# Small experts in 32-row slots, their outputs summed in PSUM expert by expert, with eleven weight slots instead of nine

## The chip, the cores and the metric

The kernel runs on one core of a Trainium2 chip. The metric is the device time of one execution in microseconds (us); lower is better. The engines are PE (TensorE), DVE (VectorE), ACT (ScalarE), POOL (GpSimd) and SP (SyncE, which here only starts the weight loads).

## The reference, cut to what matters

The model has two layers, 256 tokens of width 1024, all in fp32. Each layer has a first block (a token mixer and a mixture of 32 small experts) and a second block. The change touches the mixture of the 32 small experts. In outline:

```python
# x: [256, 1024]; E = 32 experts, hidden width F = 256, two experts per token
top2, p = route(x)                      # two expert numbers and two weights a token
y = 0
for e in range(32):
    h = silu(x @ w_gate[e]) * (x @ w_up[e])        # 1024 -> 256
    y += weight_of(token, e) * (h @ w_down[e])     # 256 -> 1024, 0 for tokens that e isn't chosen for
x = layer_norm(x * alpha + y)
```

So 512 pairs of token and expert are computed, on average 16 rows an expert. With the reference's inputs no expert gets more than 26 rows in either layer (counted from the reference's routing).

## The kernel before

All weights are streamed from HBM once. `load_weights` (L3546) issues the loads in program order on SP's queue, into `weight_ring`, RING = 9 slots of 1 MiB; a load waits until PE has used the tile that stood in its slot before. A second buffer, `weights_high` (HIGHS = 3 slots), holds the rounded high parts of those weights that are multiplied as a sum of two rounded parts, such as the projection `w_o` ahead of the experts.

Each small expert has three tiles, `moe_w_gate`, `moe_w_up` and `moe_w_down`. They are loaded in the order gate(0), up(0), then gate(x+1), up(x+1), down(x) for each x, so that the last three of the 96 are up(31) (with gate(31)), down(30) and down(31).

`sparse_experts` (L2488 on) does one mixture. The 512 pairs are ordered by expert into 512 slots. DVE makes a 0/1 matrix `G` (tokens x slots). PE transposes it to `spread` (8 products, L2590), ACT and DVE copy that out of PSUM (L2655, L2669), PE gathers the tokens' columns into the slots (`e_xg`, 32 products at L2600, of which the last 20 wait for those copies). Idle products at L130 (`idle_products`) fill PE's waits. Then `SmallExperts` (L1926) goes over the 32 experts with windows of W = 64 slots. Its PE program for step x is, in order: `first(x+1)` (half of gate and up, L1986), `turn(x)` (transposes of the hidden rows, L2007), `turn_out(x-1)` (transposes of the output rows, L2026), `second(x+1)` (the other half, L1986), `third(x)` (down, L2017). The weights are the moving operand; the x window of 64 slots is the stationary one, and two column tiles of 64 stand side by side (up and gate, or the halves of down's 1024 columns). ACT copies the hidden part (L2087), the next x window (L2094) and the output rows (L2101) and does silu (L2098, with L2096 before it, which takes a silu of one column ahead); DVE multiplies (L2134) and writes the turned output rows to `e_outT` (L2116). `by_width` reads the expert's count and branches to a wide program if the count is over W.

`sum_slots` (L2683, 32 products of one column) sums the router's weight for each slot on PE, behind the first expert's gate and up. After the last expert the engines join, and a mixing stage brings the slots back to the tokens: PE transposes `e_outT` (L2737), ACT and DVE scale each slot by its weight and split it in two rounded parts (L2762, L2769), and PE multiplies them by `spread` (L2746). DVE then adds the result to `x` (L2775, in the second layer L2777). In the second layer `meanwhile` puts a split of two tiles for the block that follows (ACT L112, DVE L116) between the join and that add.

The loops of SP, ACT and DVE over the experts are hardware loops of six experts a turn; PE's is written out.

Of the kernel before, what the change touches and what calls it, by code (L numbers as in the profile page):

```python
# [50 lines left out]
class WeightRing:  # L51
# [4 lines left out]
    def __init__(self, core):  # L56
        self.nc = core.nc
        self.buf, self.lows = core.sb_twice("weight_ring", [P, RING, SLOT])
        self.spare, self.highs = core.sb_twice("weights_high", [P, HIGHS, SLOT])
        self.full = [core.new_sem(f"weights_full_{i}") for i in range(RING)]  # L60
        self.used = core.new_sem("weights_used")
        self.high_ready, self.split_ready = core.new_sem("high_parts_ready"), core.new_sem("weights_split")
        self.loaded = [0] * RING
        self.tiles = 0
        self.split_tiles = []
        self.plan = []

    def view(self, n, kt, cols):
        return self.buf[:, n % RING, 0:kt * cols].rearrange("p (k n) -> p k n", k=kt)
# [9 lines left out]
    def next(self, src, split=False):  # L79
# [4 lines left out]
        self.tiles += 1  # L84
        self.loaded[n % RING] += 16
# [1635 lines left out]
def claim_stream(c, n, gate, up, down):  # L1721
# [6 lines left out]
    for x in range(p0, p0 + 3 * n):  # L1728
        ring.loaded[x % RING] += 16
# [198 lines left out]
class SmallExperts:  # L1928

    W = 64  # L1930

    def __init__(self, c, p0, n, unroll, xg, outT, tiles, landed, used, cnt, off):
        self.c, self.p0, self.n, self.unroll, self.xg, self.outT = c, p0, n, unroll, xg, outT
        self.gate_tile, self.down_tile = tiles
        self.landed, self.used, self.cnt, self.off = landed, used, cnt, off
        assert unroll % 2 == 0
        self.x = c.S[:, 0, :, :].rearrange("p k t -> p (k t)")[:, 0:2 * KD * self.W].rearrange("p (b k s) -> p b k s", b=2, k=KD)
        self.wide_x = c.S[:, 1, :, :]
        flat = c.xT[:, :, :].rearrange("p k t -> p (k t)")
        self.out_rows = flat[:, 0:512]  # L1940
        self.wide_hidden = flat[:, 1024:2048].rearrange("p (b m t) -> p b m t", b=2, m=2)
        spare = c.spare_x[:, :, :].rearrange("p k t -> p (k t)")
        self.hidden = spare[:, 0:2 * self.W].rearrange("p (m s) -> p m s", m=2)
        self.primed = spare[:, 640:642]
        self.squashed_rows, self.hidden_rows = spare[0:self.W, 1536:1792], spare[:, 1792:2048]
        self.wide_squashed = spare[:, 1024:1536].rearrange("p (m t) -> p m t", m=2)
        self.windowed, self.squash_done, self.rows_ready = c.sig("small_window"), c.sig("small_squashed"), c.sig("small_hidden_rows")
        self.turned, self.hidden_ready = c.sig("small_turned"), c.sig("small_hidden")
        self.rows_copied, self.out_turned, self.written = c.sig("small_rows_copied"), c.sig("small_out_turned"), c.sig("small_written")
        self.wide_act, self.wide_dve = c.sig("wide_slots_act"), c.sig("wide_slots_dve")  # L1950
        self.each = {self.windowed: 1, self.squash_done: 1, self.rows_ready: 1, self.turned: 1, self.hidden_ready: 1,
                     self.rows_copied: 1, self.out_turned: 1, self.written: 1, self.wide_act: 2, self.wide_dve: 2}
# [6 lines left out]
    def of(self, signal, x, i, part=None):  # L1959

        each = self.each[signal]
        return signal.sem, each * self.unroll * i + (self.base[signal] + each * x + (each if part is None else part))

    def load_count(self, eng, x, i):
        return eng.value_load(self.cnt[0:1, bass.ds(x + self.unroll * i, 1)], min_val=0, max_val=TOK)

    def by_width(self, eng, x, i, small, wide, count=None):

        if count is None:
            count = self.load_count(eng, x, i)  # L1970
# [5 lines left out]
    def offset(self, eng, x, i):  # L1976
        return eng.value_load(self.off[0:1, bass.ds(x + self.unroll * i, 1)], min_val=0, max_val=SLOTS)

    def gate_and_up(self, x, k0, k1):
# [10 lines left out]
    def first(self, pe, x):  # L1990
        pe.wait_ge(*self.of(self.windowed, x, 0))
        if x >= 2:
            pe.wait_ge(*self.of(self.rows_ready, x - 2, 0))
# [7 lines left out]
    def turn(self, pe, x):  # L2001
        pe.wait_ge(*self.of(self.rows_ready, x, 0))
        if x >= 2:
            pe.wait_ge(*self.of(self.hidden_ready, x - 2, 0))
        blocks = self.hidden_rows.rearrange("s (f m) -> s m f", m=2)
        for m in range(2):
            last = self.c.nc.tensor.transpose(self.c.psum[:, 2 + x % 2, m * P:(m + 1) * P], blocks[:, m, :], self.c.ident[:, :])  # L2007
        last.then_inc(self.turned.sem, 1)

    def third(self, pe, x):  # L2010
        nc, psum, W = self.c.nc, self.c.psum, self.W
        pe.wait_ge(*self.of(self.hidden_ready, x, 0))
# [8 lines left out]
    def turn_out(self, pe, x):  # L2021
        pe.wait_ge(*self.of(self.rows_copied, x, 0))
        if x >= 2:
            pe.wait_ge(*self.of(self.written, x - 2, 0))
        for j in range(4):
            last = self.c.nc.tensor.transpose(self.c.psum[:, 6 + x % 2, j * P:(j + 1) * P], self.out_rows[:, j * P:(j + 1) * P], self.c.ident[:, :])  # L2026
        last.then_inc(self.out_turned.sem, 1)

    def wide_first(self, pe, x):
        nc, psum = self.c.nc, self.c.psum  # L2030
        pe.wait_ge(*self.of(self.wide_act, x, 0, 1))
        pe.wait_ge(*self.of(self.wide_dve, x, 0, 1))
        for a, bank in ((0, 0), (1, 2)):
# [455 lines left out]

# [1274 lines left out]
```

## Time and profile before

| | |
|---|---|
| time, median of 3 runs | 2324.22 us (2323.08 to 2326.17) |
| profiled execution: own time | 2319.28 us |
| profiled execution: span | 2317.6 us |
| mean granted TensorE clock | 0.977 |
| busy: PE / DVE / ACT / POOL | 93% / 35% / 29% / 3% of the span |
| HBM read | 605.11 MB |
| chain that ended last | PE 72%, DVE 12%, DMA 8% |

The span is what the trace covers; the execution's own time is 1.7 us longer. The two mixtures of small experts lie at about 140 to 410 us and 600 to 868 us of the span. A granted clock of 1.00 is TensorE's 2.4 GHz level and 0.50 the 1.2 GHz one; a stretch between them had some of both.

### The profile page before, as it was taken

Reading aid. Unit: us, or ns where it says so; the run is one execution under the profiler, and the core shown is the slowest. Engines: PE = TensorE matmul, PEld = TensorE weight load, DVE = VectorE, ACT = ScalarE, POOL = GpSimd, SP = SyncE. Lnnn points to the kernel's source line nnn. Section 1 sums busy time; section 2 is a strip of 40 time slices with the busy share of each in tenths; the row PEclk is TensorE's granted clock in tenths of the full one; section 3 lists DMA queues with packets and bytes.
Section 4 is the critical chain, followed back from the end, with each engine's and each line's share of the span. In section 5 each row is a group of like instructions: output and inputs, shape, how many; then the busy total and the mean of one; then the engine's idle time right before and its main releaser. Section 6 shows DMA issues by size and latency. Waiting matters only on the chain.

```text
span 2317.6 us, 48110 instructions
## 1 busy us (share of the span) xinstructions
PE 2148.5 (93%) x19825; PEld 1636.9 (71%) x19825; DVE 811.6 (35%) x1483; ACT 668.6 (29%) x1151; POOL 70.3 (3%) x122
## 2 busy tenths in 40 slices
PE   7899888988998889898999998989999999999997
PEld 6775445977754559887999897876667676676775
DVE  5541112655411126974566688540000000000002
ACT  4422222453322234554333346420000000000002
POOL 0100000101000002000000200000000000000000
PEclk9999999999999999999999999999999999999999
DMA  7439999622399996333454642418999999999993
GB/s 240 143 107 419 418 419 371 185 92 76 149 418 419 419 346 175 115 128 127 146 182 147 189 164 92 146 38 326 392 371 395 379 375 400 369 377 402 364 388 123
DMA packets 196758, 610.06 MB, mean 263 GB/s; under 512 B 11472, under 2 KB 87072, under 8 KB 163728
## 3 DMA queue, kind: packets, MB, share of 16 engines
q1 hardware_dynamic: 190688, 590.84, 67.8%
q0 software_dynamic: 5248, 13.25, 2.5%
q8 instruction: 210, 3.44, 0.6%
q10 hardware_dynamic: 560, 2.10, 0.2%
q14 instruction: 52, 0.43, 0.1%
HBM read 605.11 MB, written 1.05 MB: 262 GB/s over the span
## 4 chain that ended last, share of the span: by engine, by line
PE 72%; DVE 12%; DMA 8%; ACT 3%; issue 3%; DVEq 1%; SPq 0%; ACTq 0%; POOLq 0%
PE psum L2245 18%; PE psum L2250 12%; DMA weight_ring<-in_moe_w_up_dram 8%; PE psum L1986 7%; PE psum L137 7%; PE psum L139 7%; PE psum L138 7%; PE psum L2017 2%; DVE weight_ring_rounded L116 2%; PE psum L936 1%; DVE h_cf L3165 1%; ACT scores L970 1%; PE psum L2746 1%; PE psum L2282 1%; PE psum L2026 1%
## 5 line engine op out<-in xcount | busy, mean ns | idle before, releaser
L2245 PE MATMUL psum<-weight_ring,weights_high 128*32 128x512 f32 (+2 forms) x4608 | 478.1, 470 | 0.0
L2250 PE MATMUL psum<-weight_ring,weights_high 128*32 128x256 f32 (+1 forms) x2304 | 445.5, 346 | 0.0
L1986 PE MATMUL psum<-weight_ring,scores 128*64 128x256 f32 x2048 | 259.4, 395 | 51.1 <-issue 27.4
L2250 PEld LDWEIGHTS psum<-weight_ring,weights_high 128*32 128x32 f32 x2304 | 242.7, 110 | 54.8 <-issue 1.0
L1986 PEld LDWEIGHTS psum<-weight_ring,scores 128*64 128x64 f32 x2048 | 150.6, 141 | 160.1 <-issue 111.1
L2245 PEld LDWEIGHTS psum<-weight_ring,weights_high 128*32 128x32 f32 x4608 | 184.1, 110 | 85.1 <-issue 41.1
L2250 PE MATMUL psum<-weight_ring,xT_high 128*32 128x256 f32 x1056 | 232.2, 379 | 0.0
L2245 PE MATMUL psum<-weight_ring,xT_high 128*32 128x256 f32 (+1 forms) x2112 | 231.5, 486 | 0.0
L137 PE MATMUL psum<-xT_high_rounded,weights_high_rounded 128*128 128x256 f32 x768 | 218.0, 284 | 2.2 <-DVE xT_rounded L369 1.4
L139 PE MATMUL psum<-xT_high_rounded,weight_ring_rounded 128*128 128x256 f32 x768 | 217.1, 283 | 0.0
L2354 DVE TENSOR_TENSOR xT<-xT,psum 128x768 f32<-128x768 f32 (+1 forms) x24 | 21.8, 910 | 512.4 <-PE psum L2250 374.1
L138 PE MATMUL psum<-xT_rounded,weights_high_rounded 128*128 128x256 f32 x672 | 189.1, 281 | 0.0
L116 DVE TENSOR_TENSOR weight_ring_rounded<-weight_ring,weights_high_rounded 128x2048 fp32r<-128x2048 f32 (+3 forms) x76 | 159.7, 2113 | 64.8 <-ACT weights_high_rounded L112 64.2
L2116 DVE COPY e_outT<-psum 128x512 f32 x64 | 44.3, 692 | 297.8 <-PE psum L2026 297.8
L137 PEld LDWEIGHTS psum<-xT_high_rounded,weights_high_rounded 128*128 128x128 f32 x768 | 144.9, 189 | 3.6 <-DVE xT_rounded L369 1.6
L112 ACT ACTIVATE weights_high_rounded<-weight_ring 128x2048 fp32r<-128x2048 f32 (+3 forms) x76 | 133.4, 1767 | 47.9 <-PE psum L139 41.1
L139 PEld LDWEIGHTS psum<-xT_high_rounded,weight_ring_rounded 128*128 128x128 f32 x768 | 144.5, 188 | 0.0
L2250 PEld LDWEIGHTS psum<-weight_ring,xT_high 128*32 128x32 f32 x1056 | 114.8, 110 | 37.3
L2341 ACT ACTIVATE xT_high<-psum 128x768 f32<-128x768 f32 (+1 forms) x24 | 18.6, 776 | 414.9 <-PE psum L2282 414.9
L137 PE MATMUL psum<-weights_high_rounded,xT_high_rounded 128*128 128x512 f32 (+3 forms) x336 | 122.5, 365 | 14.8 <-DVE weight_ring_rounded L116 6.5
L138 PEld LDWEIGHTS psum<-xT_rounded,weights_high_rounded 128*128 128x128 f32 x672 | 127.1, 189 | 0.5
L2017 PE MATMUL psum<-weight_ring,xT_high 128*64 128x512 f32 x512 | 121.4, 593 | 0.5 <-issue 0.4
(578 smaller groups left out, 3147.6 us busy)
## 6 DMA issues: line engine op xcount, KB each, us to landing
weight_ring<-in_moe_w_down_dram SPq DMA_DIRECT2D x152, 1024.0 KB, 9.3
weight_ring<-in_moe_w_gate_dram SPq DMA_DIRECT2D x128, 1024.0 KB, 10.0
weight_ring<-in_moe_w_up_dram SPq DMA_DIRECT2D x128, 1024.0 KB, 9.3
weight_ring<-in_moe_w_gate_dram SPq DMA_DIRECT2D x32, 768.0 KB, 6.4
weight_ring<-in_moe_w_up_dram SPq DMA_DIRECT2D x32, 768.0 KB, 4.7
weight_ring<-in_w_in_dram SPq DMA_DIRECT2D x20, 1024.0 KB, 9.3
weight_ring<-in_ffn_w_gate_dram SPq DMA_DIRECT2D x11, 1024.0 KB, 5.3
weight_ring<-in_ffn_w_up_dram SPq DMA_DIRECT2D x11, 1024.0 KB, 5.3
```

The costliest lines, as they stand in the source:

```text
L112: self.ring.nc.scalar.activation(self.high, self.whole, ACT.Copy).then_inc(self.ring.high_ready, 1)
L116: self.ring.nc.vector.tensor_tensor(self.low, self.whole, self.high.bitcast(F32), ALU.subtract).then_inc(self.ring.split_ready, 1)
L137: nc.tensor.matmul(out, lh, rh, start=start, stop=False)
L138: nc.tensor.matmul(out, lh, rl, start=False, stop=False)
L139: return nc.tensor.matmul(out, ll, rh, start=False, stop=stop)
L936: last = nc.tensor.matmul(c.psum[:, 6 + u % 2, at:at + P], PT[g % PTS][:, a * P:(a + 1) * P], wide, start=(s == 0), stop=(s == kts[j] - 1))
L970: last = nc.scalar.activation(x, x, ACT.Exp, scale=signs[u], bias=neg_max[:, u % 4, place(i):place(i) + 1], accum_out=row_sum[:, u % 4, pl ...
L1986: last = self.c.nc.tensor.matmul(psum[at:at + W, x % 2, 0:CH], self.x[:, x % 2, k, :], w[:, k, :], start=(k == 0), stop=(k == k1 - 1), ski ...
L2017: last = nc.tensor.matmul(psum[h * W:(h + 1) * W, 4 + x % 2, :], self.hidden[:, m, :], wt[:, m, h * 512:(h + 1) * 512], start=(m == 0), st ...
L2116: nc.vector.tensor_copy(self.outT[:, :, bass.ds(o, W)].rearrange("p (h j) s -> p j h s", h=2), c.psum[:, 6 + y % 2, :].rearrange("p (j h s ...
L2245: last = nc.tensor.matmul(psum[32 * q:32 * q + 32, bank + c0 // 512, 0:c1 - c0], slots(q), w[:, c0:c1], start=start, stop=stop, skip_group ...
L2250: last = nc.tensor.matmul(psum[96:P, bank + c0 // 512, at:at + rest], slots(q, True), w[:, main:], start=start and at == 0, stop=stop, ski ...
```

## The change

- **W = 32.** The window of an expert has 32 slots. Gate and up go in four column tiles of 32 (up's and gate's even and odd columns, `gate_and_up`), down in four of 256 columns (`third`).
- **Mixed at once.** For each expert DVE makes a small matrix `G` of tokens by 32 slots, already times the router's weight (`choose`), PE transposes it beside the hidden rows (`turn`), DVE copies it to `S`, ACT copies the output rows out of PSUM, and PE adds `S` times rows to the tokens' sum in PSUM banks 0 to 3, in row tiles of 32 rows (at the end of `third`). `turn_out`, the write to `e_outT`, the transposes to `spread` with their copies, `sum_slots` and the whole mixing stage are gone for the small experts.
- **Eleven slots.** `lend_highs` lends two of the three slots of `weights_high` to the expert tiles. The first two expert tiles go there, so they, and with them all behind them on SP's queue, wait until the last split product of `w_o` has used its high part.
- The loops of SP, ACT and DVE are written out. The DVE add after the experts takes its sum from banks 0 to 3, 256 columns of each.

```diff
 class SmallExperts:
-    W = 64
+    W = 32
     def gate_and_up(self, x, k0, k1):
-        gate, up = (self.c.ring.view(self.gate_tile(x) + a, KD, CH) for a in range(2))
+        gate, up = (self.c.ring.view(self.gate_tile(x) + a, KD, CH).rearrange("p k (f m) -> p k m f", m=2) for a in range(2))
         for k in range(k0, k1):
-            for w, at in ((up, 0), (gate, W)):
-                last = self.c.nc.tensor.matmul(psum[at:at + W, x % 2, 0:CH], self.x[:, x % 2, k, :], w[:, k, :],
+            for q, (w, m) in enumerate(((up, 0), (up, 1), (gate, 0), (gate, 1))):
+                last = self.c.nc.tensor.matmul(psum[q * W:(q + 1) * W, 4 + x % 2, 0:P], self.x[:, x % 2, k, :], w[:, k, m, :],
                                                start=(k == 0), stop=(k == k1 - 1), skip_group_check=(k >= KD // 2))
     def turn(self, pe, x):
...
+        pe.wait_ge(*self.of(self.rows_ready, x))
+        pe.wait_ge(*self.of(self.chosen, x))
+        if x >= 1:
+            pe.wait_ge(*self.of(self.hidden_ready, x - 1))
+            pe.wait_ge(*self.of(self.S_ready, x - 1))
+        transpose(psum[:, 6, 0:P], self.hidden_rows, self.c.ident[:, :])
+        for t in range(TT):
+            last = transpose(psum[:, 6, (1 + t) * P:(2 + t) * P], self.G[:, x % 2, t, :], self.c.ident[:, :])
     def third(self, pe, x):
...
         for m in range(2):
-            for h in range(2):
-                last = nc.tensor.matmul(psum[h * W:(h + 1) * W, 4 + x % 2, :], self.hidden[:, m, :], wt[:, m, h * 512:(h + 1) * 512],
+            for h in range(4):
+                last = nc.tensor.matmul(psum[h * W:(h + 1) * W, 7, 0:256], self.hidden[:, m, :], wt[:, m, h * 256:(h + 1) * 256],
                                         start=(m == 0), stop=(m == 1))
         last.then_inc(self.c.ring.used, 1)
+        pe.wait_ge(*self.of(self.S_ready, x))
+        pe.wait_ge(*self.of(self.rows_copied, x))
+        for t in range(TT):
+            for h in range(4):
+                last = nc.tensor.matmul(psum[:, h, t * 256:(t + 1) * 256], self.S[h * W:(h + 1) * W, x % 2, t, :],
+                                        self.rows[h * W:(h + 1) * W, x % 2, :], start=(x == 0 and t == 0), stop=(x == self.n - 1),
+                                        skip_group_check=True)
     def tensor(self, pe):
...
-            if x == 0:
-                sum_slots(pe)
...
-            if x >= 1:
-                self.turn_out(pe, x - 1)
+    def scalar(self, act, o):
+        def rows(x):
+            self.used(act, self.down_tile(x), 0)
+            copy(self.rows[:, x % 2, :], c.psum[:, 7, 0:256], ACT.Copy).then_inc(self.rows_copied.sem, 4)
+        for x in range(-2, n):
+            if x >= 0:
+                act.wait_ge(*self.of(self.turned, x))
+                copy(self.hidden, c.psum[:, 6, 0:2 * W].rearrange("p (m s) -> p m s", m=2), ACT.Copy).then_inc(self.hidden_ready.sem, 1)
+            if 0 <= x + 1 < n:
+                self.by_width(act, x + 1, lambda: act.drain().then_inc(self.wide_act.sem, 2), lambda: wide_squash(x + 1))
+            if x + 2 < n:
+                at = o if x == -2 else self.offset(act, x + 2)
+                copy(self.x[:, x % 2, :, :], self.xg[:, :, bass.ds(at, W)], ACT.Copy).then_inc(self.windowed.sem, 1)
+            if 0 <= x + 1 < n:
+                copy(self.primed[:, x % 2:x % 2 + 1], c.ones[:, 0:1], ACT.Silu)
+                self.used(act, self.gate_tile(x + 1) + 1, 0)
+                if x >= 0:
+                    act.wait_ge(*self.of(self.rows_ready, x))
+                copy(self.squashed_rows, c.psum[2 * W:4 * W, 4 + (x + 1) % 2, 0:P], ACT.Silu).then_inc(self.squash_done.sem, 1)
+            if x >= 0:
+                self.by_width(act, x, lambda: rows(x), lambda: wide_rows(x))
+        def choose(x):
...
+                last = nc.vector.tensor_scalar(self.G[:, x % 2, t, :].rearrange("p (q s) -> p q s", q=4), self.iota[:, 0:W].unsqueeze(1).broadcast_to([P, 4, W]),
+                                               self.pos[:, t, x:x + 1], self.weight[:, t, x:x + 1], ALU.is_equal, ALU.mult)
+    def lend_highs(self, p0, n):
+        extra = [RING + (len(self.split_tiles) + a) % HIGHS for a in range(2)]
+        slots = extra + [(p0 + i) % RING for i in range(RING)]
+        for slot in extra:
+            self.last[slot] = self.split_tiles[-1]
```

On PE, at one expert in the middle of the row of experts, the kernel before has these rows; L1986 is `first` and `second`, L2007 `turn`, L2026 `turn_out`, L2017 `third`, and L2037 and L2050 belong to the wide program:

```order
L1986 MATMUL psum<-weight_ring,scores 64x256 x8
L2007 MATMUL psum<-ident,xT_high 128x128 x2
L2026 MATMUL psum<-ident,xT 128x128 x4
L1971 COMPARE_AND_BRANCH
L1986 MATMUL psum<-weight_ring,scores 64x256 x8
L1971 UNCONDITIONAL_BRANCH
L2037 MATMUL psum<-scores,weight_ring 128x256 x32
L1973 UNCONDITIONAL_BRANCH
L1971 COMPARE_AND_BRANCH
L2017 MATMUL psum<-weight_ring,xT_high 64x512 x4
L1971 UNCONDITIONAL_BRANCH
```

The changed kernel has these at the same place; L2016 is `first` and `second`, L2038 the transpose of the hidden rows, L2040 those of `G`, L2052 down, L2059 the products that add to the tokens' sum, and L2075 and L2079 are wide:

```order
L2016 MATMUL psum<-weight_ring,scores 32x128 x16
L2038 MATMUL psum<-ident,xT_high 128x128
L2040 MATMUL psum<-ident,xT_high 128x128 x2
L2001 COMPARE_AND_BRANCH
L2016 MATMUL psum<-weight_ring,scores 32x128 x16
L2001 UNCONDITIONAL_BRANCH
L2075 MATMUL psum<-scores,weight_ring 128x256 x32
L2079 MATMUL psum<-ident,xT 128x128 x4
L2003 UNCONDITIONAL_BRANCH
L2001 COMPARE_AND_BRANCH
L2052 MATMUL psum<-weight_ring,xT_high 32x256 x8
L2059 MATMUL psum<-xT,xT_high 128x256 x8
```

The four transposes of output rows are gone, and behind down stand eight products that were in no such place before. (Each fp32 product here is two instructions of the trace.)

On PE, between `G` and the first expert, the rows before are these (L2590 transposes to `spread`, L2600 gathers, L130 idle products):

```order
L2590 MATMUL psum<-ident,weights_high_rounded 128x128 x8
L2600 MATMUL psum<-weights_high_rounded,scores_rounded 128x512 x32
L2687 UNCONDITIONAL_BRANCH
L130 MATMUL psum<-mask,ident 128x256 x5
L2701 UNCONDITIONAL_BRANCH
L1965 TENSOR_LOAD e_cnt_i
```

and in the changed kernel (L2694 gathers, L153 idle products):

```order
L153 MATMUL psum<-mask,ident 128x256 x8
L2694 MATMUL psum<-weights_high_rounded,scores_rounded 128x512 x32
L2791 UNCONDITIONAL_BRANCH
L153 MATMUL psum<-mask,ident 128x256 x5
L2805 UNCONDITIONAL_BRANCH
L1995 TENSOR_LOAD e_cnt_i
```

The eight transposes ahead of the gathers are gone. On SP, behind the last tile of `w_o`, the changed kernel has these rows, where the one before loads all of them into `weight_ring`:

```order
L3635 DMA weight_ring<-in_ab_w_o_dram 128x4x512 x4
L3635 DMA weights_high<-in_moe_w_gate_dram 128x2048
L3635 DMA weights_high<-in_moe_w_up_dram 128x2048
L3635 DMA weight_ring<-in_moe_w_gate_dram 128x2048
L3635 DMA weight_ring<-in_moe_w_up_dram 128x2048
L3635 DMA weight_ring<-in_moe_w_down_dram 128x2048
```

The first two expert tiles have moved to the lent slots.

## Rows read from the trace of the kernel before

**Rows 1.** The page's 40 slices of 58 us: GB/s moved

```profile
GB/s 240 143 107 419 418 419 371 185 92 76 149 418 419 419 346 175 115 128 127 146 182 147 189 164 92 146 38 326 392 371 395 379 375 400 369 377 402 364 388 123
```

**Rows 2.** Windows: busy us of each engine, granted clock, DMA share, GB/s

```profile
156.00:160.00 4.00, 4.00 (x39) 2.89 (x35) 0.41 (x1) 0.47 (x2) 0.00 (x0) 1.00 0.15 29
160.00:164.00 4.00, 4.00 (x27) 3.60 (x29) 0.16 (x1) 0.00 (x0) 0.00 (x0) 0.69 0.94 373
164.00:168.00 4.00, 4.00 (x18) 1.81 (x18) 0.00 (x0) 0.28 (x1) 0.00 (x0) 0.50 0.30 127
168.00:172.00 4.00, 4.00 (x30) 2.06 (x28) 0.41 (x1) 1.69 (x4) 0.00 (x0) 0.95 0.31 61
172.00:232.00 60.00, 55.46 (x410) 31.10 (x404) 9.95 (x18) 17.29 (x45) 0.00 (x0) 1.00 1.01 418
```

**Rows 3.** Timeline of SP's queue: start, us, transfer

```profile
120.27 0.33 SPq L3557 DMA_DIRECT2D weight_ring<-in_moe_w_gate_dram  x1
158.71 0.33 SPq L3557 DMA_DIRECT2D weight_ring<-in_moe_w_up_dram  x1
...
169.85 0.33 SPq L3557 DMA_DIRECT2D weight_ring<-in_moe_w_gate_dram  x1
```

**Rows 4.** Timeline of PE at the first experts, layer 0

```profile
142.56 1.09 PE L2590 MATMUL psum<-ident,weights_high_rounded 128*128 128x128 f32 x8 [0.79 <-DVEq L2562]
...
147.65 5.26 PE L2600 MATMUL psum<-weights_high_rounded,scores_rounded 128*128 128x512 f32 x20 [0.95 <-DVE probs_turned_rounded L2669]
...
155.00 3.67 PE L1986 MATMUL psum<-weight_ring,scores 128*64 128x256 f32 x32
158.60 4.34 PE L2683 MATMUL psum<-r_pw,e_outT 128*128 128x1 f32 x32
```

**Rows 5.** Timeline of PE at the last experts, layer 0

```profile
379.90 1.89 PE L1986 MATMUL psum<-weight_ring,scores 128*64 128x256 f32 x16
...
386.09 1.90 PE L1986 MATMUL psum<-weight_ring,scores 128*64 128x256 f32 x16
...
388.26 0.60 PE L2026 MATMUL psum<-ident,xT 128*128 128x128 f32 x4
388.79 1.95 PE L1986 MATMUL psum<-weight_ring,scores 128*64 128x256 f32 x16
```

**Rows 6.** Timeline of ACT in one expert

```profile
382.27 0.28 ACT L2087 ACTIVATE xT_high<-psum 128x128 f32<-128x128 f32 x1 [1.55 <-PE psum L2007]
383.70 0.64 ACT L2094 ACTIVATE scores<-e_xg 128x512 f32 x1 [1.16 <-issue]
...
384.59 0.38 ACT L2098 ACTIVATE xT_high<-psum 64x256 f32<-64x256 f32 x1 [0.16 <-PE psum L1986]
386.31 0.60 ACT L2101 ACTIVATE xT<-psum 128x512 f32<-128x512 f32 x1 [1.34 <-PE psum L2017]
```

**Rows 7.** Timeline of DVE: the add after the experts, layer 0

```profile
409.27 2.35 DVE L2775 SCALAR_TENSOR_TENSOR x<-x,psum 128x1024 f32<-128x1024 f32 x2 [1.06 <-PE psum L2746]
```

**Rows 8.** Costliest groups of 440 to 540 us, shapes apart

```profile
L913 PE MATMUL psum<-c_kvT,c_qT 64*128 64x256 f32 x64 | 8.8, 399 | 1.0 <-POOLq L225 1.0
...
L1577 PE MATMUL psum<-weight_ring,c_blocks 128*32 128x128 f32 x128 | 3.7, 273 | 1.3 <-DVEq L1543 1.3
```

**Rows 9.** Timelines of layer 1: SP, PE, DVE

```profile
613.43 3.67 PE L1986 MATMUL psum<-weight_ring,scores 128*64 128x256 f32 x32
...
625.16 0.33 SPq L3557 DMA_DIRECT2D weight_ring<-in_moe_w_gate_dram  x1
...
841.91 1.90 PE L1986 MATMUL psum<-weight_ring,scores 128*64 128x256 f32 x16
...
855.17 2.43 DVE L116 TENSOR_TENSOR weight_ring_rounded<-weight_ring,weights_high_rounded 128x1056 fp32r<-128x1056 f32 x2 [1.42 <-ACT weights_high_rounded L112]
...
867.02 1.22 DVE L2777 SCALAR_TENSOR_TENSOR x<-x,psum 128x1024 f32<-128x1024 f32 x1 [1.06 <-PE psum L2746]
```

**Rows 10.** A window in which PE pauses; columns as in the windows above

```profile
368.00:376.00 8.00, 4.54 (x26) 2.67 (x22) 0.00 (x0) 0.88 (x2) 0.00 (x0) 0.82 1.02 418
```

More of the change, by code:

```diff
@@ L59, in __init__ @@
         self.spare, self.highs = core.sb_twice("weights_high", [P, HIGHS, SLOT])
-        self.full = [core.new_sem(f"weights_full_{i}") for i in range(RING)]
+        self.full = [core.new_sem(f"weights_full_{i}") for i in range(RING + HIGHS)]
         self.used = core.new_sem("weights_used")
         self.high_ready, self.split_ready = core.new_sem("high_parts_ready"), core.new_sem("weights_split")
-        self.loaded = [0] * RING
+        self.loaded = [0] * (RING + HIGHS)
+        self.place, self.last, self.before, self.target = {}, {}, {}, {}
         self.tiles = 0
@@ L68, in view, with take_slot @@
     def view(self, n, kt, cols):
-        return self.buf[:, n % RING, 0:kt * cols].rearrange("p (k n) -> p k n", k=kt)
+        slot = self.place.get(n, n % RING)
+        part = self.buf[:, slot, 0:kt * cols] if slot < RING else self.spare[:, slot - RING, 0:kt * cols]
+        return part.rearrange("p (k n) -> p k n", k=kt)
+    def take_slot(self, n, slot):
+        self.before[n] = self.last.get(slot)
+        self.last[slot] = n
+    def lend_highs(self, p0, n):
[3 more added lines that the diff above has]
+            self.last[slot] = self.split_tiles[-1]
+        for i in range(n):
+            slot = slots[i % len(slots)]
+            self.place[p0 + i] = slot
+            self.take_slot(p0 + i, slot)
+            self.loaded[slot] += 16
+            self.target[p0 + i] = (self.full[slot], self.loaded[slot])
     def low(self, n, kt, cols):
@@ L2135, in vector_step @@
-        if after_rows:
-            after_rows(dve)
-        if x >= 1:
-            write(x - 1)
-        if 0 <= x + 1 < n:
-            self.by_width(dve, x + 1, i, lambda: dve.drain().then_inc(self.wide_dve.sem, 2), wide_combine)
-    def steps(self, eng, step, begin, end):
-        start = 2
-        turns = (self.n - 2 - start) // self.unroll
-        for x in range(begin, start):
-            step(eng, x, 0)
-        with eng.Fori(0, turns) as i:
-            for x in range(start, start + self.unroll):
-                step(eng, x, i)
-        for x in range(start + turns * self.unroll, end):
-            step(eng, x, 0)
@@ L3557, in load, with load_once @@
             sp.dma_start(ring.view(dst_n, kt, cols), src).then_inc(ring.full[dst_n % RING], 16)
+        def load_once(n, src):
+            if ring.before[n] is not None:
+                sp.wait_ge(ring.used, ring.before[n] + 1)
+            kt, cols = src.shape[1:]
+            sp.dma_start(ring.view(n, kt, cols), src).then_inc(ring.full[ring.place.get(n, n % RING)], 16)
         for entry in ring.plan:
@@ L3561, in _ @@
                 _, n, dst, src = entry
-                load(n, 0, n, src)
+                load_once(n, src)
                 continue
@@ L3570, in expert @@
                     tile = lambda at, src: load(far + at, i, at, src)
-                    if ahead:
-                        if x + 1 < n:
-                            tile(p0 + 2 + 3 * x, gate(e + 1, 0))
-                            tile(p0 + 3 + 3 * x, up(e + 1, 0))
-                        tile(p0 + 2 + 3 * x + (2 if x + 1 < n else 0), down(e, 0))
-                        return
                     for q, src in enumerate(way.sources(e, gate, up, down)):
@@ L3579, in _ @@
                 if ahead:
-                    load(p0, 0, p0, gate(0, 0))
-                    load(p0 + 1, 0, p0 + 1, up(0, 0))
+                    load_once(p0, gate(0, 0))
+                    load_once(p0 + 1, up(0, 0))
+                    for x in range(n):
+                        if x + 1 < n:
+                            load_once(p0 + 2 + 3 * x, gate(x + 1, 0))
+                            load_once(p0 + 3 + 3 * x, up(x + 1, 0))
+                        load_once(p0 + 2 + 3 * x + (2 if x + 1 < n else 0), down(x, 0))
+                    continue
                 with sp.Fori(0, turns) as i:
```

653 lines of the change are left out of this document (342 added, 311 removed).

## The prediction

> **What bounds the kernel now.** I first read the page's slices [rows 1]. Two stretches stand out, the slices from 174 to 348 us and from 638 to 811 us: 418 to 419 GB/s, flat. Both lie in the mixtures of small experts; the slices between the two move 76 to 371. Windows over the first of them [rows 2] say the same, 418 GB/s at a DMA share of 1.01 from 172 us on. So the middle of a mixture is bound by the weight stream: a tile of 1.049 MB at 418 GB/s takes 2.51 us, an expert's three take 7.5.
>
> What PE needs when tiles are there is less: at the end of layer 0 the first half of expert 30's gate and up starts at 379.90 and that of expert 31 at 386.09 [rows 5], 6.2 us an expert. So in the middle PE waits for loads, and shortening its work there brings nothing. What counts is when the stream becomes saturated, and what comes after its last tiles.
>
> The start, from SP's queue [rows 3] and PE [rows 4]: nine tiles are loaded ahead, the ninth issued at 120.27. The next load is issued at 158.71, when expert 0's gate and up are used (PE 155.00 plus 3.67), and the twelfth tile (number 11, counted from 0) only at 169.85, since PE first does the 32 one-column products of `sum_slots` (4.34 us) and then runs at the lower clock (0.50 in 164 to 168 [rows 2]). The DMA runs dry meanwhile: 29 GB/s in 156 to 160, 127 and 61 in 164 to 172. In layer 1 PE starts at 613.43, and tile 11 is issued at 625.16 [rows 9].
>
> The end: expert 31's gate and up start on PE at 386.09 [rows 5], the add begins at 409.27 [rows 7], 23.2 us later. In layer 1 it is 841.91 to 867.02, 25.1 us [rows 9].
>
> **The change, part by part.**
>
> *Start of the stream.* Gone ahead of the gathers: eight transposes (142.56 at 1.09 us, of which some 0.85 counts, since the next products start under their end) and the gathers' stall of 0.95 us for the copies [rows 4]. With the refilling of PE's queue I take 2.3 us, bounds 1.8 and 2.8: expert 0 starts at 152.7. Its gate and up are 64 instructions in rounds of four column tiles of 32. The same shape stands in L1577, 128 instructions in 3.7 us busy [rows 8], 0.116 us a round: 16 rounds are 1.85 us. The moving operand is now read with a step of two; I give it 0.2 us, bounds 0 and 1.85 (half speed). So PE is through at 154.8 instead of 158.67, and there is no `sum_slots` behind it. With eleven slots tiles 0 to 10 have been loaded since 120.27 (27.6 us at 2.51, done by 148), and what is issued at 154.9 is tile 11: against 169.85, **14.9 us earlier**. A check by bytes: from 156.5 to 172 the stream at 418 GB/s moves 6.5 MB, where the four windows [rows 2] moved 2.4; 4.1 MB are 9.9 us, and two more tiles ahead are 5.0, together 14.9. Layer 1: 613.43 - 2.3 + 2.1 = 613.2 against 625.16 [rows 9], **12.0 us earlier**.
>
> The expert tiles that were loaded earlier than 120.27 are now loaded behind it, for their slots are free only after the last product of `w_o` [rows 3]. That costs nothing while the eleventh lands (148) ahead of expert 0 (152.7), which leaves 4.7 us; without that cover each us of lateness costs one.
>
> *In the middle.* Does the new chain stay under 7.5 us? ACT and PE now hand work back and forth. On ACT [rows 6], for one expert: hidden copy 0.28; two register reads with a branch, 1.16 of issue; window copy and L2096, 0.89 from start to start, 0.7 with half the window; silu 0.38, 0.3 for half the columns; another read and branch, half of the 1.16, 0.6; copy of the rows 0.4 (128x512 took 0.60): 3.4 us. Then on PE, until ACT can go on: the mixing products, `first` of the next expert (0.95, half of 1.85) and `turn`, six instructions for 0.4 (eight take 0.53 to the next row, [rows 5]). The mixing products are 16 instructions of 32 rows by 256 columns, and no 32-row tile is in the trace. With no overlap they would be as `third` or `first` instructions of 256 columns two by two: 386.09's 16 take 1.90 in pairs [rows 5], so 3.4 to 3.8 singly; with all four row tiles at once 0.9. L913, two row tiles of 64 rows, has 64 instructions in 8.8 us [rows 8], 2.2 for 16, and shows that row tiles do overlap by two. I take 0.9 (as the four column tiles, which L1577 shows do overlap), and keep 2.2 as the bound of the main case. Sum: 3.4 + 0.9 + 0.95 + 0.4 and four hand-overs at 0.15: **6.3 us**, and 7.6 at the upper bound; the slack is 1.2. DVE's part (two `choose`, product, `S` copy of 128 to 256 columns; the add's 1.2 us for 1024 columns [rows 7] puts the four under 2 us together) runs beside it.
>
> The Trainium skill, "TensorE: Matmul & The Clock Gate", Part 3 (Measured speedup), has four row tiles of K = 32 at 3.07 times one; no run here shows it yet. By it the 16 products take some 1.2 us and the period is 6.6. A rule that speaks against the change stands in the Trainium skill under "TensorEngine Tiling (Array Packing)", Key Properties: a change of tiling mode drains TensorE, and an expert now has four such changes where it had two. In this trace the four transposes of L2026 and the change behind them take 0.53 us together [rows 5], so a change hides in under 0.2 us, and two more are 0.4 at most, inside the slack.
>
> *End.* From the start of expert 31's gate and up: `first` 0.95, `turn(30)` 0.4, `second` 0.95, `third(30)` 0.9, wait for ACT's rows 0.7, mix 0.9, `turn(31)` 0.4, hidden copy 0.4, `third(31)` 0.9 (down(31) lands two tiles, 5 us, behind up(31)), rows copy with its branch 1.2, mix 0.9, join and branches 2.1: 10.7 us to the add (bounds 9.5 and 14) against 23.2, **12.5 us less**; in place of output transposes, writes and the mixing stage stand the two mixes. In layer 1 `meanwhile`'s split, which before lay partly under the mixing, stands alone between join and add: ACT's first tile and DVE's two (2.43 from 855.17, 1.1 behind ACT's start, [rows 9]), 3.5 us. So 14.2 against 25.1, **10.9 us less**.
>
> *What follows.* The next block's tiles stand in the same stream and move with it. I take 0.7 us a layer off for the code of the loops now written out, fetched over the same DMA, and 1 us for a gain vector or another small load that isn't moved: 2.4 us lost, bounds 0 and 6.
>
> Sum: 14.9 + 12.5 + 12.0 + 10.9 - 2.4 = **47.9 us gained**. The profiled execution's own time of 2319.28 becomes 2271.4; the median of the runs is 4.9 above that execution, so I predict **2276 us**.
>
> **The rivals.**
>
> *B, the chain comes near the stream's pace.* Mixing products at 2.2 us or hand-overs at 0.4 each bring the period to 7.6 to 7.8. At 7.7 the start's gain is eaten by 31 x 0.2 = 6 us a layer, and the tail grows with each step, by 3 us a layer: 2294. At 7.85 nothing but little is left, 2310. Or the gain in the stream isn't kept since PE starts later than I take it (the lent slots late, code fetched in the way): with half of 26.9 lost, 2290. So 2290 to 2319. For it: a long chain of short steps with ACT twice in it. Against: most bounds lie under 7.5.
>
> *C, slower: the chain becomes the bound.* Place: each expert. If the row tiles don't overlap (3.4 us) the period is 8.8. Expert 31 then starts at 154.8 + 31 x 8.8 = 427.6 instead of 386.1, and the tail gives back 12.5 - 5: +34 us in layer 0 and some more in layer 1, 2390. It decides from (386.1 + 12.5 - 154.8) / 31 = 7.86 us, 7.73 in layer 1. The granted clock can do the same: in 368 to 376, behind one long pause, PE is busy 4.54 of 8 us and has 0.82 [rows 10], and in 164 to 168, behind one-column products, it has 0.50 [rows 2]. The new kernel keeps PE busy for only about 4.3 of 7.5 us throughout. At 0.50 the 2.3 us of PE work on the chain double, the period is 8.6, time 2370. Against: the pauses are short and spread, and a slower PE fills them. The Trainium skill states the gate as a rule ("TensorE: Matmul & The Clock Gate", Part 1): a TensorE that idles is put to its lower clock. Rows 10 agree as far as they go.
>
> *D, no change:* a period just at 7.8.
>
> **How the numbers follow.** Main case 0.66, with its own range 2262 to 2290 from the bounds above. B 0.19, C 0.12, D 0.03. The main case and three quarters of B lie in 2260 to 2308. A measurement of this kernel tells 0.2% (4.6 us) from no change. Faster 0.85, same 0.03, slower 0.12.
>
> **What would show it.** In the changed profile: tile 11 issued near 155 and 613; over 400 GB/s from there to the last expert tile; PE's waits in the middle ended by the loads, not by ACT; 16 mixing instructions in 0.9 to 1.2 us; the first add near 382 and that of layer 1 near 844; the add 11 and 14 us behind expert 31's first product. I am wrong if PE's steps are over 7.7 us apart with a DMA share under 1, if the granted clock stays under 0.8 in the mixtures, or if expert 0 waits for its tiles.

## The result, and the profile after

The changed kernel takes 2411.59 us (median of 4 runs, 2405.37 to 2412.91) where the kernel before takes 2323.65 (4 runs beside it): a ratio of 1.0379, 95% interval 1.0357 to 1.0401. It is 88 us slower; I had predicted 2276 us and gave "slower" 12%.

The page of the changed kernel: the slices of 60 us with granted clock and GB/s, the instruction queue of PE's code (packets, MB), and the chain that ended last by engine.

```profile
PEclk9998787898988878999999999999999999999999
GB/s 224 21 358 343 334 342 335 171 93 22 241 342 348 342 328 237 170 101 157 88 183 184 159 166 123 123 123 159 358 388 392 368 389 390 370 385 393 368 387 135
...
q8 instruction: 246, 4.03, 0.7%
...
PE 74%; DVE 11%; issue 8%; ACT 4%; DVEq 1%; ACTq 1%; DMA 1%; PEld 0%; PEldq 0%; POOLq 0%
```

Where the kernel before has 418 to 419 GB/s [rows 1], this one has 328 to 348. The stream no longer sets the pace in the mixtures. In the chain DMA fell from 8% to 1%, and "issue", waits for nothing that the profile shows, rose from 3% to 8%. Nearly all that changed in time lies in these two mixtures: the add behind the first comes 38.9 us later than before and the add behind the second 88.7 (955.75 against 867.02 [rows 9]), of 91.6 us in the span.

The start went as predicted. PE and SP at the first expert, layer 0:

```profile
142.17 8.22 PE L2694 MATMUL psum<-weights_high_rounded,scores_rounded 128*128 128x512 f32 x32 [0.78 <-DVEq L2647]
150.23 2.32 PE L153 MATMUL psum<-mask,ident 128*128 128x256 f32 x10
152.48 2.03 PE L2016 MATMUL psum<-weights_high,scores 128*32 128x128 f32 x64
...
154.57 0.33 SPq L3635 DMA_DIRECT2D weights_high<-in_moe_w_gate_dram  x1
```

Expert 0 starts at 152.48 (was 155.00, [rows 4]), its 64 instructions take 2.03, and tile 11 is issued at 154.57, where it was 169.85 [rows 3]. The windows that follow (columns as in [rows 2]) show the loss:

```profile
172.00:232.00 60.00, 40.24 (x657) 26.97 (x661) 7.32 (x24) 8.95 (x32) 0.00 (x0) 0.86 0.87 348
232.00:292.00 60.00, 41.30 (x644) 26.89 (x637) 8.47 (x28) 9.59 (x35) 0.00 (x0) 0.77 0.85 330
292.00:352.00 60.00, 39.87 (x629) 26.27 (x629) 7.35 (x25) 8.35 (x30) 0.00 (x0) 0.80 0.86 338
```

DMA share 0.85 to 0.87 and 330 to 348 GB/s, PE busy for 40 to 41 of 60 us, clock 0.77 to 0.86. PE's timeline for two experts in the second of them:

```profile
263.06 1.17 PE L2052 MATMUL psum<-weight_ring,xT_high 128*32 128x256 f32 x16
264.88 1.15 PE L2059 MATMUL psum<-xT,xT_high 32*128 32x256 f32 x16 [0.65 <-ACT xT L2130]
267.44 1.14 PE L2016 MATMUL psum<-weight_ring,scores 128*32 128x128 f32 x32 [1.41 <-issue]
268.51 0.33 PE L2038 MATMUL psum<-ident,xT_high 128*128 128x128 f32 x1
268.67 0.38 PE L2040 MATMUL psum<-ident,xT_high 128*128 128x128 f32 x2
268.99 1.12 PE L2016 MATMUL psum<-weight_ring,scores 128*32 128x128 f32 x32
272.95 1.40 PE L2052 MATMUL psum<-weight_ring,xT_high 128*32 128x256 f32 x16 [2.85 <-issue]
274.99 2.09 PE L2059 MATMUL psum<-xT,xT_high 32*128 32x256 f32 x16 [0.63 <-ACT xT L2130]
277.01 0.64 PE L2016 MATMUL psum<-weight_ring,scores 128*32 128x128 f32 x2
279.36 1.93 PE L2016 MATMUL psum<-weight_ring,scores 128*32 128x128 f32 x30 [1.72 <-issue]
```

The 16 mixing instructions (L2059) take 1.15 us, so the row tiles overlap, and their wait for ACT is 0.65 us. What costs are three pauses "issue" of 1.41, 2.85 and 1.72 us. They stand behind branches, or in the middle of a row of 32 like instructions (16 products); behind the 2.85 the clock is lower and the same products take 1.93 instead of 1.12. The transpose of the hidden rows (in `turn`) stands once in each expert, and gives the step from one expert to the next:

```profile
L2038 PE MATMUL psum<-ident,xT_high x32: 327/372/476, 155.8 to 442.0; 128*128 128x128 f32 x32
```

That is 9.2 us on the mean of 31 steps, where 7.5 would keep pace with the stream. The waits of PE over 175 to 437 us (us in total, times, longest):

```profile
PE psum L2052 <- issue: 29.9, 16, 4.6
PE psum L2016 <- issue: 28.6, 17, 3.7
...
PE psum L2059 <- issue: 8.1, 5, 2.4
```

Together 66.6 us in 28 experts, 2.4 us each. The add follows at 448.12 (was 409.27, [rows 7]):

```profile
448.12 2.35 DVE L2846 SCALAR_TENSOR_TENSOR x<-x,psum 128x1024 f32<-128x1024 f32 x2 [4.82 <-POOLq L248]
```

### The profile page after: what moved, and what is told of

The parts are those of the page before. It is cut to its first block, busy times and chain, and to the rows that moved or that the text cites. A ratio compares the mean times of both kernels' runs of the same rounds, so it can differ in the third digit from the quotient of the medians.

```text
span 2409.2 us, 53784 instructions
## 1 busy us (share of the span) xinstructions
PE 2100.7 (87%) x23009; PEld 1642.0 (68%) x23009; DVE 805.6 (33%) x1592; ACT 620.4 (26%) x1132; POOL 70.3 (3%) x122
## 3 DMA queue, kind: packets, MB, share of 16 engines
q8 instruction: 246, 4.03, 0.7%
## 4 chain that ended last, share of the span: by engine, by line
PE 74%; DVE 11%; issue 8%; ACT 4%; DVEq 1%; ACTq 1%; DMA 1%; PEld 0%; PEldq 0%; POOLq 0%
PE psum L2276 17%; PE psum L2281 12%; PE psum L2016 7%; PE psum L160 7%; PE psum L162 6%; PE psum L161 6%; PE psum L2059 4%; PE psum L2052 3%; DVE weight_ring_rounded L139 2%; PE psum L959 2%; DVE h_cf L3236 1%; ACT xT L2130 1%; PE psum L2694 1%; PE psum L153 1%; PE psum L2038 1%
## 5 line engine op out<-in xcount | busy, mean ns | idle before, releaser
L2016 PE MATMUL psum<-weight_ring,scores 128*32 128x128 f32 x3264 | 167.3, 336 | 56.0 <-issue 55.0
L2016 PEld LDWEIGHTS psum<-weight_ring,scores 128*32 128x32 f32 x3264 | 122.8, 132 | 98.7 <-issue 95.0
L2190 DVE COPY xT_high<-psum 128x256 f32<-128x256 f32 x64 | 27.1, 424 | 399.5 <-ACT xT_high L2141 399.5
L2059 PE MATMUL psum<-xT,xT_high 32*128 32x256 f32 x1024 | 96.4, 476 | 59.3 <-ACT xT L2130 44.8
L2059 PEld LDWEIGHTS psum<-xT,xT_high 32*128 32x128 f32 x1024 | 60.5, 219 | 98.1 <-issue 96.3
```

The lines of the kernel that those rows point to most:

```text
L2016: last = self.c.nc.tensor.matmul(psum[q * W:(q + 1) * W, 4 + x % 2, 0:P], self.x[:, x % 2, k, :], w[:, k, m, :], start=(k == 0), stop=(k = ...
L2059: last = nc.tensor.matmul(psum[:, h, t * 256:(t + 1) * 256], self.S[h * W:(h + 1) * W, x % 2, t, :], self.rows[h * W:(h + 1) * W, x % 2, : ...
L2190: nc.vector.tensor_copy(self.S[:, x % 2].rearrange("p t s -> p (t s)"), c.psum[:, 6, P:3 * P]).then_inc(self.S_ready.sem, 1)
```

## What could make PE pause: code

In the trace the instruction queue q8 brings blocks (16.4 KB each, 4.03 MB in 246), and a block of it lands near the end of nearly every long pause: in 20 of the 22 pauses over 1 us between 170 and 370 us one lands 1.3 to 2.4 us before the products go on. PE's program holds for each expert the small form and the wide one that is jumped over. Each product is four instructions (two weight loads, two matmuls), each transpose two. Before: 26 products and transposes small (6 of them transposes) and 48 wide an expert. Changed: 51 small (32 for gate and up, 3 transposes, 8 and 8) and 60 wide (4 of them transposes). With the waits and branches, the row of instructions that PE passes or jumps over grew from some 300 to some 440 an expert.

The Trainium skill has something on this under "Runtime: NRT & Kernel Launch", Instruction fetch mechanics: code comes in blocks of 256 instructions by a DMA queue of the engine's own, in sequence, and a taken branch out of what is held makes the engine wait. I had not weighed that page of the Trainium skill in the prediction. The experiments test it (theory F) against three rivals: H, hand-overs with ACT and short pauses that keep the clock low; J, the branch itself; and C of the prediction, row tiles that don't overlap, which the 1.15 us above already rule out.

## The experiments

**1. The wide code taken out of PE's program.** In `tensor`, in the changed kernel:

```diff
-                following = self.load_count(pe, x + 1)
                 self.first(pe, x + 1)
...
-                self.by_width(pe, x + 1, lambda: self.second(pe, x + 1), lambda: self.wide_first(pe, x + 1), following)
+                self.second(pe, x + 1)
...
-                self.by_width(pe, x, lambda: self.third(pe, x), lambda: self.wide_third(pe, x), count)
+                self.third(pe, x)
```

> The changed kernel with PE's wide program, its count reads and its branches left out (no expert of these inputs is wide, so the same products run). Theory F (code fetch: PE jumps over some 240 instructions of wide code for each expert and then waits for its next code block): the waits of 1.8 to 5.2 us that the trace of the changed kernel ends by issue go away, the step falls from 9.2 us to the 7.5 of the weight stream, the granted clock in the mixtures rises over 0.95, time 2265 to 2285. Rival H (hand-overs with ACT and short pauses hold PE at the lower clock): only the branch costs go, some 0.3 us of 9.2 a step, time over 2385, clock under 0.87 as now.

Measured: 2268.15 us (4 runs, 2263.59 to 2273.42), ratio to before 0.9762 (0.9732 to 0.9792). A window of it, its instruction queue, its waits over 175 to 370 us, and its first add:

```profile
232.00:292.00 60.00, 42.82 (x792) 29.67 (x780) 9.74 (x32) 11.14 (x40) 0.00 (x0) 0.89 1.01 419
```

```profile
q8 instruction: 185, 3.03, 0.5%
```

```profile
PE psum L2016 <- DMA weight_ring<-in_moe_w_up_dram: 27.5, 17, 2.5
PE psum L2059 <- ACT xT L2129: 22.6, 27, 1.2
...
PE psum L2016 <- DMA weights_high<-in_moe_w_up_dram: 4.3, 3, 1.9
```

```profile
379.90 2.35 DVE L2845 SCALAR_TENSOR_TENSOR x<-x,psum 128x1024 f32<-128x1024 f32 x2 [3.07 <-POOLq L248]
```

The stream is full again (419 GB/s), PE waits for loads and no longer by "issue", and the same products that took 2411 us now take 2268. The clock is 0.89, not over 0.95 as I had expected, and costs nothing, since the stream sets the pace. H falls: the hand-overs (0.84 us an expert) and the short pauses are all still there. 246 - 185 = 61 blocks less in 64 experts are 244 instructions an expert at 256 a block: the wide form has 56 products and 4 transposes, 232 instructions, and with it went its waits, the reads of the counts and the branches.

**2. The branches kept, only the code behind them out.** `with pe.If(count < self.W + 1)` with no `Else`, the counts read as before.

> As the first, but PE still reads each count and branches; only the wide code that it would jump over is left out. Theory F (size of the code jumped over): within 10 us of the first kernel. Rival J (the branch itself stalls PE, whatever lies behind it): as the changed kernel, over 2385. Theory H: over 2385 too.

Measured: 2266.65 us (2261.07 to 2271.59), ratio 0.9762 (0.9728 to 0.9796), 186 blocks. As experiment 1: reading a count and branching cost nothing here. J falls. One window of this run (232 to 292 us) has a granted clock of 0.84 at 419 GB/s, so a clock as low as the changed kernel's doesn't by itself hold up the stream.

**3. The same in the kernel before.** The edit of experiment 1.

> The kernel before with PE's wide program and branches left out in the same way. Theory F: its single pauses of 2.2 to 3.5 us (some four to six a mixture) go, but the stream bounds the middle, so it gains only where a pause let the DMA run dry: 2305 to 2322. H: no change, 2324.

Measured: 2314.55 us (10 runs, 2307.02 to 2316.21), ratio 0.9963 (0.995 to 0.9977), 160 blocks where the kernel before has 210. Wide code and branches cost the kernel before 0.4% too, small but clear of the noise.

**4. Code added to the kernel before, and nothing else.** In `wide_third`, which never runs with these inputs:

```diff
-        for k in range(KD):
+        for k in [k for _ in range(3) for k in range(KD)]:
```

> The kernel before with the never executed wide down program written three times over on PE, so that an expert's code on PE is about as long as in the changed kernel (some 430 instructions, where it was 300); nothing else changes, and not one more product runs. Theory F: PE gets pauses as in the changed kernel and the step goes over the stream's 7.5 us: 2350 to 2430. H and J: 2324, within 0.3%.

Measured: 2416.44 us (2412.74 to 2418.02), ratio 1.0404 (1.0373 to 1.0434). The old kernel, with W = 64 and none of the change, is as slow as the changed one. The instruction queue of the kernel before, and this run's instruction queue, one window and PE's timeline:

```profile
q8 instruction: 210, 3.44, 0.6%
```

```profile
q8 instruction: 242, 3.96, 0.7%
```

```profile
232.00:292.00 60.00, 46.48 (x306) 25.58 (x305) 7.74 (x14) 13.73 (x35) 0.00 (x0) 0.94 0.90 363
```

```profile
278.04 0.60 PE L2026 MATMUL psum<-ident,xT 128*128 128x128 f32 x4
278.57 1.95 PE L1986 MATMUL psum<-weight_ring,scores 128*64 128x256 f32 x16
280.35 1.89 PE L2017 MATMUL psum<-weight_ring,xT_high 128*64 128x512 f32 x8
283.70 1.95 PE L1986 MATMUL psum<-weight_ring,scores 128*64 128x256 f32 x16 [1.46 <-issue]
```

128 instructions more an expert are 8192 in the two mixtures, and 242 - 210 = 32 blocks: 256 instructions a block, as that page of the Trainium skill has it, and every added block, though only jumped over, was brought in. The step is 8.7 us (163.9 to 433.8 for 31 steps), where the kernel before has 7.3 (166.5 to 392.4). The clock stays at 0.94 here and the time is lost all the same. In the changed kernel the clock is lower, 0.80 over 175 to 437 us, and rises to 0.90 (175 to 370 us of experiment 1) when nothing but the code is taken out: the lower clock follows from the pauses and adds to them, but doesn't start the loss.

**5. Far more of it.** As 4, with `range(12)`.

> The kernel before with the never executed wide down program written twelve times over on PE (three times in the fat one): 576 more instructions an expert to jump over, 144 more blocks of 256 instructions over both mixtures. Nothing more is computed. Theory V (every block of code is brought in, also one that is only jumped over, one after another, and that row of blocks sets the pace): 242 + 144 = 386 blocks in the instruction queue, at the 3.1 to 5.3 us a block of the fat run 2.25 more blocks an expert, so 7 to 12 us more a step: 2860 to 3160. Theory T (only the block of the target is brought in): no more than 2 blocks and 3 to 5 us an expert, as the fat run: 2400 to 2480, with about 242 blocks.

Measured: 2593.39 us (1 run), 317 blocks. Both theories miss: V said 386 blocks and over 2860, T about 242 and under 2480. 75 of the 144 added blocks were brought in. A jump over nearly 800 instructions thus spares part of the blocks, and what still comes costs: the step is 11.6 us on the mean (162.8 to 523.0 for 31 steps).

**6. One decision a mixture.** DVE takes the largest count; PE reads it once. `tensor_any` is the old body of `tensor`.

```diff
     def tensor(self, pe):
+        widest = pe.value_load(self.widest, min_val=0, max_val=TOK)
+        with pe.If(widest < self.W + 1):
+            for x in range(-1, self.n):
+                if x + 1 < self.n:
+                    self.first(pe, x + 1)
+                if x >= 0:
+                    self.turn(pe, x)
+                if x + 1 < self.n:
+                    self.second(pe, x + 1)
+                if x >= 0:
+                    self.third(pe, x)
+        with pe.Else():
+            self.tensor_any(pe)
...
+            c.dve(nc.vector.tensor_reduce(most[:, :], cnt[:, :], AX_X, ALU.max))
+            nc.vector.tensor_copy(widest[:, :], most[0:1, :])
```

> The changed kernel with all it can do, but PE decides once a mixture: DVE takes the largest count, PE reads it and runs either 32 experts without any wide code, or the old row of programs with both forms, which then is jumped over whole (some 15,000 instructions, 59 blocks). Theory T: as the small-only kernel, 2265 to 2280. Theory V, if it holds for any distance: 59 blocks at 3.1 to 5.3 us behind each mixture, 180 to 310 us twice, 2620 to 2890.

Measured: 2271.74 us (2267.68 to 2280.86), ratio 0.9782 (0.9744 to 0.9821), faster than both kernels and with all the changed kernel can do.

```profile
q8 instruction: 189, 3.10, 0.5%
```

Four blocks more than in experiment 1: the jump over the old row of programs (some 14,000 instructions by the 440 an expert, 55 blocks a mixture; I had expected 59) doesn't bring them in. T holds for a far jump, V for a near one. The far jump isn't free, though. The last mixing products of layer 0 on PE, and the add on DVE:

```profile
374.20 1.15 PE L2060 MATMUL psum<-xT,xT_high 32*128 32x256 f32 x16 [0.66 <-ACT xT L2146]
```

```profile
379.64 2.35 DVE L2866 SCALAR_TENSOR_TENSOR x<-x,psum 128x1024 f32<-128x1024 f32 x2 [6.76 <-POOLq L248]
```

From the end of the products to the add it is 4.3 us, where experiment 1 has 0.6; in layer 1 9.2 against 3.8. A block of code is brought in in between (from 376.7 and from 811.4 us). So the jump at the end costs 3.7 and 5.4 us, once a mixture and not in each expert. In these two profiled executions it hardly shows in the time of the add (379.64 against 379.90), because expert 0 starts 1.7 us earlier here (150.46 against 152.15); why is open.

**7. Only the wide down program out** (96 instructions an expert), by the edit of experiment 2 at `third` alone.

> The changed kernel with only the wide down program left out on PE (96 of some 250 jumped-over instructions an expert). Both code theories: 370 instructions or 1.45 blocks an expert at the 5.3 us that a block took in the changed kernel: a step of 7.7 us, so near the stream's pace, 2275 to 2320. Theory H: 2400.

Measured: 2354.69 us (2354.16 to 2363.31), ratio 1.0144 (1.0109 to 1.0179), 221 blocks. Slower by 35 us than the upper end of what I expected. The steps are 5.5 to 12.3 us, 8.6 on the mean of 28 from 170.9 to 411.4, with 39 blocks in them: one every 6.2 us, not the 5.3 that I had carried over, at some 350 instructions an expert. A time for each block, held constant, is too simple; the direction is right.

**8. Nine slots instead of eleven**, in the kernel of experiment 1 (`extra = []` in `lend_highs`).

> The small-only kernel with nine slots for the expert tiles instead of eleven; the loads still wait for w_o's last product. By the prediction's account the two tiles ahead are worth 2 x 2.51 = 5.0 us a mixture: 10 us slower than small-only, 2278. Rival: the ring is no matter once the code is out of the way (PE catches up in the middle), within 3 us of 2268.

Measured: 2276.82 us (2273.1 to 2278.1), ratio 0.9793 (0.9763 to 0.9822) beside 0.9762. 8.7 us between the medians, near what the account of the two tiles says (10.0); the intervals of the ratios overlap, so the size is not settled, only likely. In the two traces the first add comes 3.9 us later (383.75 against 379.90) and that of layer 1 6.4 (821.50 against 815.09). Against what I wrote ahead of the run, the edit also undoes the wait for `w_o`: the first tiles are again loaded ahead, as in the kernel before, up to the ninth at 120.05. That wait was covered in any case, so the difference is still that of the two tiles.

**9. One decision on PE, ACT and DVE alike.**

> The changed kernel with the one decision a mixture on PE, ACT and DVE alike: ACT's two branches an expert go too. If the middle is bound by the weight stream at 7.5 us a step, ACT's 1.2 us a step bring nothing there and only the tail of each mixture gets shorter, by 1 to 2 us: 2264 to 2272. If ACT's chain still holds the steps, more: under 2260.

Measured: 2274.12 us (2272.64 to 2274.81), ratio 0.9792 (0.977 to 0.9814). No gain over experiment 6, and 2 us over the range that I expected: in the middle ACT's branches are not what anything waits for. Even the tail brought nothing (first add at 379.82, against 379.64): the wait behind the last mixing products, 4.3 us in experiment 6, is 4.6 here.

**10. The weight stream thinned, all code kept.** Behind the first eleven tiles of a mixture a quarter of each expert tile is loaded:

```diff
+                        rows, width = (kt, cols) if m < p0 + 11 else (2, cols) if kt == KD else (1, cols // 2)
+                        sp.dma_start(ring.view(m, kt, cols)[:, 0:rows, 0:width], src[:, 0:rows, 0:width])
```

> The changed kernel, all wide code kept, but behind the first eleven tiles of a mixture only a quarter of each expert tile is loaded (the rest of the slot keeps old weights, so the output of the experts is not the reference's). Theory Q (a code block is slow to arrive because it stands behind the weight packets on the same DMA engines): blocks come at 2.5 us or less, PE's pauses shrink, step 5.8 to 6.5. Theory R (a block takes its 3 to 5 us whatever else the DMA carries): step 8.5 to 9.5 as in the changed kernel, 2380 to 2410.

The rest of each slot keeps old weights, so this run serves for times alone. Measured: 2274.72 us (1 run). Its window of 172 to 340 us, and the instruction queue of 170 to 340:

```profile
172.00:340.00 168.00, 124.64 (x2425) 85.39 (x2426) 30.00 (x99) 33.79 (x121) 0.00 (x0) 0.97 0.38 122
```

```profile
q8 instruction: 43, 0.70, 1.7%
```

A block every 3.95 us, where the changed kernel has 49 in 175 to 437, one every 5.35. The step is 6.8 us, between the two theories and nearer to Q. The pauses over 1 us between 170 and 370 us sum to 22.6 us here and to 45.3 in the changed kernel. So the load that the weights put on the DMA explains most of the loss, 9.2 to 6.8, in part by way of the clock, which is 0.97. How it does so isn't shown: the transfer of a block itself takes 1.0 us (median) in both traces. And it isn't all: two blocks in a row stand 3.1 us apart at the least in both traces, and 6.8 is still above the 5.5 that PE has without the wide code.

## Why the prediction was wrong

**The step that failed** is "In the middle": the new chain's 6.3 us an expert, and with it the chance of 0.66. It summed what ACT and PE execute and left out what PE has to fetch. Measured without the wide code the chain is even shorter, 5.5 us (the first steps of experiment 1), so the sum as a whole was large enough, though its mixing term was not (0.9 against 1.15). The pauses by code added 2.4 us; what remains to 9.2, some 1.3, I put down to the lower clock behind them and the rest of the waits, an estimate by difference. The "What follows" term gave 0.7 us a layer to the code of the loops written out, those of SP, ACT and DVE, as bytes on the DMA. PE's own code, half as long again an expert, stood in no term of the main case; rival B has "code fetched in the way" in half a sentence, as a later start. It isn't the bytes but PE's wait for the next block. The sign of being wrong that the prediction names came about as written: steps over 7.7 us (9.2) at a DMA share under 1 (0.84).

**Rival C** had the right sign and the right point of decision (7.86 and 7.73 us), with the wrong mechanisms; that its 8.8 and 2390 lie near the measured 9.2 and 2412 is chance. Row tiles overlap four at a time (1.15 us for 16 instructions; 3.4 was the bound without), in accord with the Trainium skill, "TensorE: Matmul & The Clock Gate", Part 3, whose ratio gave some 1.2. The clock did fall, to 0.77 to 0.86; experiment 4 shows the loss at a clock of 0.94, experiments 1 and 2 show 0.89 and 0.84 costing nothing.

**Start of the stream:** right. 152.48 (predicted 152.7), 2.03 us for gate and up (2.1), tile 11 at 154.57 (154.9).

**Tiling modes:** no cost seen; where the tiles are there, the rows of L2059, L2016 and L2038 follow each other without idle time in experiment 1.

**The end:** right once the code is out. In experiment 1 the add begins at 379.90 (predicted near 382), 29.4 us earlier than before (27.4). Expert 31's gate and up start at 368.98, 10.9 us ahead of it (10.7), and in layer 1 at 799.68, 15.4 ahead (14.2). In layer 1 DVE shows the split alone ahead of the add, as said:

```profile
812.75 2.43 DVE L139 TENSOR_TENSOR weight_ring_rounded<-weight_ring,weights_high_rounded 128x1056 fp32r<-128x1056 f32 x2 [3.90 <-ACT weights_high_rounded L135]
815.09 1.21 DVE L2847 SCALAR_TENSOR_TENSOR x<-x,psum 128x1024 f32<-128x1024 f32 x1
...
826.06 1.23 DVE L3063 TENSOR_TENSOR scores<-x,cat 128x1024 f32<-128x1024 f32 x1 [1.67 <-DMA cat<-in_norm_mix_w_dram]
```

815.09 against 867.02 [rows 9] is 51.9 us, 22.6 of them in layer 1 (22.9 predicted). The prediction's marks for layer 1, tile 11 near 613 and the add near 844, leave out that layer 0 moves it all by 27.4; with it they are 585.8 and 816.7, and experiment 1 has 584.78 and 815.09. The last of these rows is the small load that comes late (1.67 us). In all 53 us were gained in the medians (2321.36 to 2268.15) where I had summed 47.9. Some of that is luck: 6.8 of the 53 are what the kernel before itself lost to its wide code (experiment 3). Beside that kernel without its wide code the gain is 46.4 us by the medians (2314.55 to 2268.15), and 44.4 at the add of layer 1 (859.44 to 815.09) where the parts sum to 50.3. So the part of the working that deals with loads and tail holds to some 12%, and the whole forecast failed at one resource that it didn't price.

**What stays open:** what a block costs as a rule (one comes every 3.95 to 6.2 us where code slows the step), why two blocks in a row stand 3.1 us apart in experiments 4 and 10 and the changed kernel but often less than 1 us in experiment 5, and from how far a jump spares the blocks between (none spared at 320 instructions jumped over an expert, half of the added ones at some 900, nearly all at some 14,000).

## What to carry to other kernels

Count an engine's instructions for each turn of the work, those that a branch jumps over too, and hold the row of blocks (256 instructions each) against the step time; with the DMA full, here the limit lay between 300 instructions in 7.5 us, which cost 0.4%, and some 350, which cost 3.8% (experiment 7 beside experiment 1). A rare form that is written out beside the common one in every turn can be paid in every turn: decide once ahead of the loop and put the rare program far away, where the jump over it is paid once. A PE wait that the profile calls "issue" and that stands behind a branch or within a row of like products is a sign to look at the instruction queue before looking at the engines.

## What the runs showed that I had not expected

- Code that never ran cost 4.0% (experiment 4: 32 more blocks, 2321.36 to 2416.44 us, 3 us for each block added).
- The granted clock fell with the pauses by code and rose when they went: 0.80 in the changed kernel (175 to 437 us), 0.90 in experiment 1 (175 to 370 us), with the same products.
- A far jump over some 14,000 instructions brings in next to none of their blocks and holds up the end of a mixture by 4 to 5 us, which the times of the whole (2271.74 beside 2268.15 us) don't show clear of the noise.
